# Modulation weights split in two rounded parts and multiplied in two f32r passes, in a two-layer hybrid mixer kernel

## The reference

```python
mod_lat = (jax.nn.silu(c) @ w_ada[l] + b_ada[l])[:, None, :]      # w_ada[l]: 1024 x 3072
mod_ctx = jax.nn.silu(c_ctx) @ w_ada[l] + b_ada[l]
u_c, gate_c = adaln_modulate(h_ctx, mod_ctx)                       # layer_norm(h) * (1 + scale) + shift
u_x, gate_x = adaln_modulate(h_lat, mod_lat)
pc, px = split_proj(u_c @ w_in[l]), split_proj(u_x @ w_in[l])
```

## Time and profile before

| what | value |
|---|---|
| runs | 2919.88, 2899.03, 2919.62 us; median 2919.62 us |
| profiled execution | span 2913.2 us on its one core; no device time of its own is given beside the span |
| TensorE busy | 2752.0 us (94%) |
| VectorE, ScalarE, GpSimd busy | 1542.9, 1008.1, 640.3 us |
| mean granted TensorE clock | 0.982 |
| opening of layer 0 | about 0 to 143 us of the span |
| opening of layer 1 | about 1624 to 1728 us |

### The profile page before, as it was taken

How to read it: one execution, slowest core, us unless ns; L and a number is a source line. 1 busy time by engine, 2 the same in 40 slices (tenths; PEclk the granted TensorE clock), 3 DMA queues, 4 the chain that set the end, 5 groups by cost and what they waited for, 6 DMA issues and landing times.

```text
span 2913.2 us, 50304 instructions
## 1 busy us (share of the span) xinstructions
PE 2752.0 (94%) x21254; PEld 2160.7 (74%) x21254; DVE 1542.9 (53%) x2691; ACT 1008.1 (35%) x1640; POOL 640.3 (22%) x261
## 2 busy tenths in 40 slices
PE   7999998999999999999999999888899999999997
PEld 1387877887788888887787448777776787887775
DVE  4646676425624443436747644667524554352856
ACT  0335443312222343224432134544332233432533
POOL 0022000121123211320124312100132342142036
PEclk9999999999999999999999999999999999999999
DMA  7521000323332112220134651000233331232034
GB/s 230 173 78 43 16 19 24 107 77 116 96 118 87 59 51 103 79 80 30 48 109 157 199 185 58 30 14 14 74 109 119 128 129 55 89 121 69 23 116 166
DMA packets 104958, 261.95 MB, mean 90 GB/s; under 512 B 11202, under 2 KB 33860, under 8 KB 104352
## 3 DMA queue, kind: packets, MB, share of 16 engines
q1 hardware_dynamic: 94314, 231.07, 24.1%
q10 hardware_dynamic: 10422, 27.67, 2.6%
HBM read 217.27 MB, written 34.08 MB: 86 GB/s over the span
## 4 chain that ended last, share of the span: by engine, by line
PE 77%; DVE 13%; ACT 4%; DMA 3%; issue 3%; POOL 1%; DVEq 0%; SPq 0%; ACTq 0%
PE ps L823 17%; PE ps L824 16%; PE ps L825 16%; PE ps L1003 4%; PE ps L831 4%; PE ps L1330 4%; PE ps L962 2%; PE ps L1269 2%; PE ps L1357 2%; PE ps L840 2%; DVE t_gcv L1979 1%; PE ps L1340 1%; PE ps L917 1%; PE ps L946 1%; DMA t_raw<-in_w_ada 1%
## 5 line engine op out<-in xcount | busy, mean ns | idle before, releaser
L784 POOL TENSOR_TENSOR t_wlo<-t_raw,t_whi 128x1024 fp32r<-128x1024 f32 x248 | 618.5, 2496 | 2242.0 <-ACT t_whi L1451 2242.0
L823 PE MATMUL ps<-t_u_hi,t_whi 128*128 128x512 f32 (+1 forms) x2368 | 862.4, 364 | 10.5 <-issue 4.1
L824 PE MATMUL ps<-t_u_lo,t_whi 128*128 128x512 f32 (+1 forms) x2368 | 834.6, 352 | 0.0
L825 PE MATMUL ps<-t_u_hi,t_wlo 128*128 128x512 f32 (+1 forms) x2368 | 831.2, 351 | 0.0
L1451 ACT ACTIVATE t_whi<-t_raw 128x1024 fp32r<-128x1024 f32 x248 | 262.4, 1058 | 890.9 <-PE ps L825 687.4
L823 PEld LDWEIGHTS ps<-t_u_hi,t_whi 128*128 128x128 f32 x2368 | 449.8, 190 | 83.1 <-issue 18.2
L825 PEld LDWEIGHTS ps<-t_u_hi,t_wlo 128*128 128x128 f32 x2368 | 448.0, 189 | 63.3
L824 PEld LDWEIGHTS ps<-t_u_lo,t_whi 128*128 128x128 f32 x2368 | 450.1, 190 | 58.5 <-issue 3.4
L1522 ACT ACTIVATE t_grp<-ps 128x512 f32<-128x512 f32 (+2 forms) x236 | 104.3, 466 | 228.7 <-PE ps L840 107.0
L2514 DVE TENSOR_REDUCE t_amx<-ps 128x1 f32<-128x768 f32 (+1 forms) x120 | 101.5, 846 | 149.2 <-PE ps L1330 148.6
L1971 DVE TENSOR_TENSOR t_yv<-t_oT,t_sil 128x768 f32<-128x768 f32 (+1 forms) x32 | 67.1, 2097 | 184.2 <-ACT t_sil L1522 184.2
(11 more groups left out here) (267 smaller groups left out, 3865.7 us busy)
## 6 DMA issues: line engine op xcount, KB each, us to landing
t_raw<-in_w_in SPq DMA_DIRECT2D x184, 512.0 KB, 3.6
t_raw<-in_w_ada SPq DMA_DIRECT2D x48, 512.0 KB, 4.4
t_raw<-in_w_br SPq DMA_DIRECT2D x32, 512.0 KB, 3.6
t_raw<-in_w_out SPq DMA_DIRECT2D x32, 512.0 KB, 4.2
t_sg<-gate_logits SPq DMA_DIRECT2D x28, 384.0 KB, 4.2
hs<-t_hstage ACTq DMA_DIRECT2D x20, 512.0 KB, 3.6
t_hring<-hs SPq DMA_DIRECT2D x20, 512.0 KB, 6.6
t_raw<-in_fwd SPq DMA_DIRECT2D x64, 128.0 KB, 3.0
```

The lines of the kernel that those rows point to most:

```text
L784: pool.tensor_tensor(wlo[:, c % CONV, :], raw[:, s % RAW, :], whi[:, c % CONV, :].bitcast(f32), ALU.subtract).then_inc(sems["w_ready"], 1)
L823: pe.matmul(o, lh, rh, start=first, stop=False)
L824: pe.matmul(o, lh, rl, start=False, stop=False)
L825: return pe.matmul(o, ll, rh, start=False, stop=last)
```

## The change

Pieces of `w_ada` become converted pieces. The conditioning vector is split as well: `cs_parts` holds, for each 128 rows, two rounded columns and two remainder columns side by side. For each 128 rows TensorE multiplies the four columns by the rounded weights, and then the two rounded columns by the remainder of the weights, into the same accumulators. The result has four rows; rows 2 and 3 (remainder columns) are added by the "turn", which is now a product with `sel` of four rows instead of a transpose, and for the gate rows by the existing products with `sel`. `row` first copies four rows and then adds the bias to two. ScalarE calls `pieces_used` for "ada" pieces where it only counted them before, and `splits_due` once ahead of the loop. GpSimd's six additions of layer 0's end are placed at several points of the stream. The masks are loaded in four transfers of the parts that are used, and cast by one instruction.

```diff
@@ -261,13 +261,15 @@
 
 
 STREAM = [(l, *x) for l in range(DEPTH) for x in stream_of(l)]
-IS_RAW = [x[1] in ("ada", "fwd", "inv") for x in STREAM]
+IS_RAW = [x[1] in ("fwd", "inv") for x in STREAM]
 CONV_AT = [i for i, r in enumerate(IS_RAW) if not r]
 CONV_OF = {s: c for c, s in enumerate(CONV_AT)}
 RAW_DMAS = [4 if x[1] == "fwd" else 1 for x in STREAM]
 RAW_DUE = [16 * sum(RAW_DMAS[s % RAW:s + 1:RAW]) for s in range(len(STREAM))]
 INV_AT = [i for i, x in enumerate(STREAM) if x[1] == "inv"]
 LAYER_AT = [sum(x[0] < l for x in STREAM) for l in range(DEPTH)]
+ADDS_BEHIND = {LAYER_AT[1] - 1: (0, 1, 2), STREAM.index((1, "ada", 2, 0)): (3,), STREAM.index((1, "ada", 2, 1)): (4,),
+               STREAM.index((1, "ada", 3, 1)): (5,), len(STREAM) - 1: tuple(range(LT - 1))}
 
 
 class Lane:
@@ -366,16 +368,15 @@
         acc_f = acc[:, :].rearrange("p (k t) -> p k t", k=KT)
         acc_t = acc[:, :].rearrange("p (i d) -> p i d", i=NT)
         raw = sb("raw", [P, RAW, 1024])
-        with ExitStack() as m:
-            mask_f = sb("mask_f", [P, 2 * LEVELS * P], stack=m)
         whi, wlo = sb("whi", [P, CONV, 1024], f32r), sb("wlo", [P, CONV, 1024], f32r)
         cst = sb("cst", [P, 8, P])
         masks = sb("masks", [P, 2, LEVELS - 1, 64], u8)
         par = sb("par", [P, NPAR])
         mod = sb("mod", [P, 16, 2])
-        grow = sb("grow", [2, D])
-        sel = sb("sel", [2, 2, P])
+        grow = sb("grow", [4, D])
+        sel = sb("sel", [4, 2, P])
         cs = sb("cs", [P, KT, 2])
+        cs_parts = sb("cs_parts", [P, KT, 4], f32r)
         oT = sb("oT", [P, BT, TOK])
         bst = sb("bst", [P, NT, 2, 6])
         mv = sb("mv", [P, NT, 2])
@@ -403,10 +404,11 @@
         with ExitStack() as m:
             sd = sb("sd", [P, 2, 2, 4, BW], stack=m)
             sd_ctx = sb("sd_ctx", [P, 2, 2, 2, BW], stack=m)
-            mrow = sb("mrow", [2, 2, 512], stack=m)
+            mrow = sb("mrow", [4, 2, 512], stack=m)
             bada = sb("bada", [2, 2, 512], stack=m)
             hstage = sb("hstage", [P, 2, 2, 1024], stack=m)
             craw = sb("craw", [P, KT, 2], stack=m)
+            mask_f = sb("mask_f", [P, 2, LEVELS - 1, 64], stack=m)
         dec = early[:, 0:NT * BW].rearrange("p (i w) -> p i w", i=NT)
         hyb = early[0:1, 3072:4096]
         row0 = early[0:1, 4096:4096 + BW]
@@ -783,12 +785,10 @@
                 pool.wait_ge(sems["w_hi"], c + 1)
                 pool.tensor_tensor(wlo[:, c % CONV, :], raw[:, s % RAW, :], whi[:, c % CONV, :].bitcast(f32),
                                    ALU.subtract).then_inc(sems["w_ready"], 1)
-                l = STREAM[s][0]
-                if s + 1 == len(STREAM) or STREAM[s + 1][0] != l:
-                    for i in range(NT if l == 0 else LT - 1):
-                        pool.wait_ge(sems["wo_g"], (NT if l else 0) + i + 1)
-                        pool.tensor_tensor(acc_t[:, i, :], acc_t[:, i, :], lng[:, 1, :], ALU.add)\
-                            .then_inc(sems["wo_out"], 1)
+                for i in ADDS_BEHIND.get(s, ()):
+                    pool.wait_ge(sems["wo_g"], (NT if s + 1 == len(STREAM) else 0) + i + 1)
+                    pool.tensor_tensor(acc_t[:, i, :], acc_t[:, i, :], lng[:, 1, :], ALU.add)\
+                        .then_inc(sems["wo_out"], 1)
 
 
         @block.tensor
@@ -953,24 +953,25 @@
                         network(l, a, 2)
                     if kind == "ada":
                         if a == 0 and b == 0 and l == 0:
-                            ln.take("ada_silu")
+                            ln.take("ada_silu", 2)
                         if b == 0:
                             claim(6 + a % 2)
-                        r, _ = piece()
+                        hi, lo = piece()
                         for kk in range(2):
-                            k = 2 * b + kk
-                            last = pe.matmul(ps[0:2, 6 + a % 2, :], cs[:, k, :], r[:, kk * 512:(kk + 1) * 512],
-                                             start=k == 0, stop=k == KT - 1)
+                            k, c = 2 * b + kk, slice(kk * 512, (kk + 1) * 512)
+                            pe.matmul(ps[0:4, 6 + a % 2, :], cs_parts[:, k, :], hi[:, c], start=k == 0, stop=False)
+                            last = pe.matmul(ps[0:2, 6 + a % 2, :], cs_parts[:, k, 0:2], lo[:, c],
+                                             start=False, stop=k == KT - 1)
                         ln.done(last, "stream_used")
                         if b == 3:
                             lend("ada_row", 6 + a % 2)
                     if kind == "turn":
                         if a == 0 and l == 0:
-                            pe.wait_ge(sems["ld_const"], 32)
+                            pe.wait_ge(sems["ld_const"], 48)
                         claim(6 + a % 2)
                         for j in range(4):
-                            last = pe.transpose(ps[:, 6 + a % 2, 2 * j:2 * j + 2], mrow[0:2, a % 2, j * P:(j + 1) * P],
-                                                cst[0:2, C_ID, 0:2])
+                            last = pe.matmul(ps[:, 6 + a % 2, 2 * j:2 * j + 2], mrow[:, a % 2, j * P:(j + 1) * P],
+                                             sel[:, :, 0], start=True, stop=True)
                         ln.done(last, "ada_t")
                         lend("ada_mod", 6 + a % 2)
                     if kind == "tap":
@@ -1543,12 +1544,15 @@
             def open_layer(l):
                 if l == 0:
                     act.wait_ge(sems["ld_c"], 16)
-                    ln.done(run(cs[:, :, :], craw[:, :, :], ACT.Silu), "ada_silu")
+                    ln.step(run(cs[:, :, :], craw[:, :, :], ACT.Silu), "act_step")
+                    ln.done(run(cs_parts[:, :, 0:2], cs[:, :, :], ACT.Copy), "ada_silu")
                     act.dma_start(cst[:, :, :], A["cst"]).then_inc(sems["ld_const"], 16)
-                    act.dma_start(sel[:, :, :], A["sel"]).then_inc(sems["ld_const"], 16)
+                    for i in range(2):
+                        act.dma_start(sel[2 * i:2 * i + 2, :, :], A["sel"]).then_inc(sems["ld_const"], 16)
                     for dst, src in filter_inputs(l):
                         act.dma_start(dst, src).then_inc(sems["ld_filter"], 16)
                     act.wait_ge(sems["ld_par"], 16)
+                    splits_due()
                 for kind, a, b in opening(l):
                     if kind == "net":
                         sine(l, a)
@@ -1556,8 +1560,13 @@
                             for i in range(NT):
                                 act.dma_start(acc_t[:, i, :], residual(l, i)).then_inc(sems["ld_h"], 16)
                         if a == 2:
-                            act.dma_start(mask_f[:, :], A["masks"]).then_inc(sems["ld_c"], 16)
-                    if kind in ("ada", "blk"):
+                            full = A["masks"].rearrange("p (a b c) -> p a b c", a=2, b=LEVELS)
+                            for r in near:
+                                for x in range(2):
+                                    act.dma_start(mask_f[r, x, :, :], full[r, x, 0:LEVELS - 1, r]).then_inc(sems["ld_c"], 16)
+                    if kind == "ada":
+                        pieces_used()
+                    if kind == "blk":
                         ln.skip(1)
                         used[0] += 1
                     if kind == "blk":
@@ -1585,7 +1594,7 @@
                             ln.take("wo_out")
                             act.dma_start(A["h1"][P * a:P * a + P, :], acc_t[:, a, :]).then_inc(sems["st_h"], 16)
                         elif a == 0:
-                            act.wait_ge(sems["ld_const"], 32)
+                            act.wait_ge(sems["ld_const"], 48)
                         deviation(mv[:, a, 1:2], rstd[:, a:a + 1])
                     if kind == "unit":
                         if l and a == 0:
@@ -2009,7 +2018,8 @@
 
                 dve.wait_ge(bada_ld[n % 2], 16 * (3 * l + n // 2 + 1))
                 dst = mrow[:, n % 2, :] if n < 4 else grow[:, (n - 4) * 512:(n - 3) * 512]
-                ln.done(tt(dst, ps[0:2, 6 + n % 2, :], bada[:, n % 2, :], ALU.add), "ada_row")
+                step(dve.tensor_copy(dst, ps[0:4, 6 + n % 2, :]))
+                ln.done(tt(dst[0:2, :], ps[0:2, 6 + n % 2, :], bada[:, n % 2, :], ALU.add), "ada_row")
 
             def modulation(n):
 
@@ -2065,6 +2075,9 @@
 
             def open_layer(l):
                 g = groups(l)
+                if l == 0:
+                    ln.take("ada_silu")
+                    ln.done(tt(cs_parts[:, :, 2:4], cs[:, :, :], cs_parts[:, :, 0:2].bitcast(f32), ALU.subtract), "ada_silu")
                 dve.wait_ge(sems["ld_par"], 16 * (l + 1))
 
                 def taps(x, t):
@@ -2092,11 +2105,10 @@
                     if kind == "w4":
                         sum_weights(l)
                     if kind == "masks":
-                        dve.wait_ge(sems["ld_c"], 32)
```

(4 more changed lines are left out.)

## The result

The changed kernel takes **2979.23 us** (median of 4 runs, 2976.8 to 2985.14); the kernel before, on the same chip, 2917.27. The ratio is 1.0226, with a 95% interval of 1.019 to 1.0261: 62 us slower, where 12 were forecast. The profiled execution has a span of 2979.0, 65.8 more than before. In these tables an opening's length is read from TensorE's timeline.

The account below looks back on a forecast made before the run. The bound was taken to be delivery of pieces (transfer, rounding, GpSimd's subtraction), with TensorE barely setting the pace beside taps. Layer 0 +4, layer 1 +7 and contention +1 gave +12: span 2925, time 2931 us, range 2920 to 2943.

Parts of the forecast that it names:

- TensorE still sets the pace there, barely: Beside taps: a tap with a new piece takes 2.9 us, against GpSimd's 2.4 to 2.5 a piece.
- 12 x 0.86 = **-10.3: Rest of layer 0: twelve pieces between taps and transforms, TensorE bound, each win 0.86 us.
- its like in layer 1: Layer 1's tap stretch: taps win back only 1.7 us, with GpSimd's additions between the pieces.
- The step of 0.24 us: New w_ada products: an f32r product of 512 columns takes 0.24 us, four in a piece 0.95.
- Head of layer 0: +13 forecast: Layer 0 up to the first tap: supply and ScalarE's queue move the first tap from 50.41 to 63.4 us.
- Layer 1: +7 forecast: Layer 1's opening: late pieces, rows and turns, and ScalarE's wait before the token tiles add 7 us.
- rival 1: Both openings: supply keeps up, with roundings three pieces ahead; -19 us, 2901; chance 0.22.
- rival 2: Layer 1's opening and layer 0's reductions: VectorE and GpSimd block each other, 3.7 us a piece; 2954; chance 0.11.
- where 1 was counted: Layer 0's reductions and weights' sums: VectorE meeting GpSimd costs +1 to +4 us, taken as +1.
- Rival 3: Fp32 taps and transforms: more waits put 20 to 30 us of them at a lower clock; 2955; chance 0.07.
- layer 1's waits today cost no clock: Layer 1: offered as the argument against a loss of 20 to 30 us through a lower clock.
- Rival 4: New w_ada products: four narrow columns cost as fp32 for 28 pieces with taps or transposes; +24, 2955; chance 0.03.

Follow-up runs that it names:

- e7: Changed kernel, but the w_ada blocks beside each layer's first taps stay raw with fp32 products: 2966.65 us, ratio 1.0171.
- e14: Changed kernel with every f32r product beside the first taps issued twice, the extra into a bank nobody reads: 2970.53 us, ratio 1.0182.
- e6: Changed kernel with one idle fp32 product ahead of each w_ada piece between the first four taps of either layer: 2975.63 us, ratio 1.0204.
- e15: Kernel before, with the bias row copied five more times ahead of each layer's first taps to make a wait; usual two fp32 products: 2928.95 us, ratio 1.0048.
- e16: Kernel before with the same made wait, but only one fp32 product per piece beside the first taps: 2943.7 us, ratio 1.0095.
- e17: Kernel before with the same made wait, and four f32r products per piece in layer 1's third block, raw supply: 2942.1 us, ratio 1.0082.
- e3: Changed kernel, but ScalarE rounds no w_in piece in the openings until the tokens are on their way: 2967.35 us, ratio 1.0195.
- e2: Changed kernel, but GpSimd subtracts only 16 of 1024 columns of every w_ada piece from the fourth on: 2945.78 us, ratio 1.0122.
- e11: Changed kernel with raw pieces beside the first taps, w_in roundings after the tokens, and layer 0's later sines after the next block's third piece: 2951.68 us, ratio 1.013.
- e10: Kernel before, leaving out one of each piece's two fp32 products beside the first taps: 2916.4 us against 2913.47, ratio 1.001.
- e13: Kernel before, raw supply, with four f32r products replacing each piece's two fp32 ones in layer 1's third block: 2915.32 us, ratio 1.0011.
- e12: Changed kernel converting only covered pieces, w_in after tokens; beside first taps one fp32 product of rounded weights replaces four f32r: 2935.11 us, ratio 1.0074.
- e4: The change in layer 0 alone; layer 1's w_ada pieces raw with fp32 products as before: 2951.36 us, ratio 1.0141.
- e5: Changed kernel converting only layer 0's blocks 3 to 5 and layer 1's blocks 2 and 3, w_in roundings after the tokens: 2939.87 us, ratio 1.0083.
- e8: Changed kernel converting only layer 0's blocks 4 and 5 and layer 1's block 3, w_in after the tokens: 2914.61 us against 2912.86, ratio 1.0007.

## Why the prediction was wrong

**The failed step.** "TensorE still sets the pace there, barely" and the sum behind it, "12 x 0.86 = **-10.3**", and its like in layer 1, took every product, tap and transform at full clock. The step of 0.24 us for an f32r product is right where the clock is up (103.99, 104.22, 104.45), and wrong where it counted: beside the first taps it is 0.43. From the first tap to the end of the first transform the sums have 2.6 us less in layer 0 (four pieces at 0.86, against the longer row and turn) and 0.8 less in layer 1 (1.7, against one row and turn); measured are +10.1 and +10.9. That is some 24 us of the 54 between the span that was forecast, 2925, and the one measured. Rows of the same form at either level price it: a tap steps by 3.71 instead of 1.92, a piece by 1.80 instead of 1.02, the turn by 1.80 instead of 0.98, and the transforms take 6.31 and 8.69 instead of 3.70 and 7.13. By these half clock costs 13.7 us in layer 0's stretch and 12.7 in layer 1's. That work beside the taps decides is shown by e7 and e14, which take 5 to 6 us from layer 0's opening and 2 to 6 from layer 1's with more work in them, by e6 in layer 0, and by e15 against e16 and e17. The change both lowers the clock (late pieces, 10.91 and 1.49 before the first tap) and shortens the product behind which it used to return.

**Head of layer 0: +13 forecast, +20.0 measured.** The steps up to the second sine were right: first product 17 forecast, 16.81 measured; sine near 36, 36.94; roundings from 39, 40.04. The third sine came at 58.98, not 54. Its rows: the weights' sums took 6.4 us instead of 3.3, a sum and the copy being held up by GpSimd, and `row` has a wait and a pass more. The last piece's products were through at 67.0, not 61. From there row and turn took 3.4, not 2.4: the row wait is 1.49 instead of 0.77, and the turn, allowed 0.2 more, went from 0.41 to 1.86, eight records at half clock instead of four.

**Layer 1: +7 forecast, +31 measured.** The first product comes 3.5 us after the last one of layer 0, as counted. The eighth piece is 8.7 late where 7 were forecast, GpSimd taking 2.61 a piece for the first seven; row and turn in front of the first tap add most of the rest of the 10.1. The tap stretch then loses some 12 to the forecast, as said. The first transposed tokens are 23.5 late (forecast 8), and from there to the end another 7.4 go, where 1 was to come back: ScalarE had been waiting for transfers, then normed six tokens in a row, and TensorE waits 2.54 and 4.49 for modulated tokens, partly at half clock. (Two waits of 1.42 stand there too, but they were 1.41 before.) Ahead of the 4.49 ScalarE rounded a w_in piece at 1770.13, for whose transfer it had waited 4.55, with the tokens behind it. e3, which moves that rounding, takes 2.5 us from layer 1's opening; the rest was not divided up.

**Where the gain came.** Between the first transform and the last piece of layer 0 the clock is up, and so is the gain: -4.7 for eight pieces, where 6.2 were forecast (eight pieces at 0.86, against one longer row). The wait that follows it (2.36 before, 6.89 after) takes it back: ScalarE stood at 148.50 for a w_in transfer with the tokens behind it in its queue. Such a wait was forecast for layer 1 and missed in layer 0.

**The rivals.** The supply did not keep up (rival 1). GpSimd's subtractions took 2.3 to 2.8 each in the openings, not 3.7, so rival 2's lock did not set the pace; but VectorE lost 4.7 us to it on the way to the second and third sine (1.5, 1.2 and 2.1), where 1 was counted. Rival 3, the clock, is what happened, at about the size that it named (20 to 30 us; by the rows above 26), and had 7 in 100. Its time, 2955, still lies 24 us short, since the supply's terms were too small as well. The argument against it, "layer 1's waits today cost no clock", was the error: those waits were shorter than the new ones and stood in front of long products, and the change alters both. Rival 4 did not occur: four narrow columns step as 16 do.

The 62 us in sum: of the 63 that the openings grew by, e2 takes 28 away with GpSimd's time and e3 some 6 with ScalarE's order; half clock beside the first taps and at the first transforms is 26 by its rows, of which e7 recovers 12. These overlap; e11, with three mends, recovers 29. How the loss divides exactly stays open.

## What to carry to other kernels

Before making a product shorter, look at what stands on either side of it: where the granted clock has just fallen, the long product may be what brings it back, and half the work can take longer (e16 against e15). Price a stretch at both clocks whenever the change makes a wait in front of it. A piece that moves from "transfer, use" to "transfer, round, subtract, use" costs its slowest station wherever less than that time of other work lies beside it, and costs again in whatever stands behind the rounding in the same queue.

## What the runs showed that was not expected

- TensorE stays at 1.2 GHz while busy without a pause: 22 us (70.45 to 92.55), taps of 3.78 with f32r work of 1.7 between them. In e16 the same with fp32 work of 1.87. With 3.5 (e14) or 3.57 (e7, e15), and in e6's layer 0 with a filler and the f32r behind it, the clock came back by the second tap. In e6's layer 1 it did not: 3.7 us passed and the second tap took 3.78, so the length of the product is not the whole rule. Whether taps, with 64 rows, count for less than products with 128 was not tried apart.
- At full clock it stayed full with 0.95 of fp32 (e10) or 1.01 of f32r (e13) between four taps.
- The fall itself is not tied to one length of wait. Waits of 2.6 in e10 and e13 and of 4.3 in e15 to e17 were each followed by one, and a wait of 2.52 ahead of a piece in e12's layer 0 (45.70) was not: the four taps behind it stayed at 1.99 or just below.
- The new turn may lower the clock by itself. In e4, e5, e8 and e12 layer 1 has raw pieces ahead of its first tap and the old wait of 0.77, but the turn with `sel`: eight records in 1.05 instead of four in 0.41. In all four the clock falls within the first tap (2.70, 3.09, 3.07, 3.18). With the old turn behind the same wait (before, e10, e13) that tap takes 1.99. No run changes the turn alone (in those four the raw products also have two more columns, of zeros), and in layer 0 of e5, e8 and e12 the first tap stayed at 1.99. So this is not shown. Layer 1 before, then e12:

```profile
1641.87 0.40 PE L972 MATMUL ps<-t_cst,t_mrow 2*128 2x2 f32 x4 [0.78 <-DVE t_mrow L1971]
1642.20 1.99 PE L946 MATMUL ps<-t_net 64*128 64x512 f32 x4
...
1640.89 1.05 PE L985 MATMUL ps<-t_sel,t_mrow 2*128 2x2 f32 x8 [0.77 <-DVE t_mrow L1999]
```

- A VectorE instruction with a single SBUF input is held up by GpSimd too: 0.55 became 2.02, 0.68 became 2.74.
